# A drain on GpSimd in the expert loop of an encoder layer, between the gathers and the scatter

## The chip, the core and the metric

The kernel runs on one core of a Trainium2 chip. A core has five engines that run their own instruction streams and meet through semaphores: TensorE (PE in the profile, its weight loads PEld), VectorE (DVE), ScalarE (ACT), GpSimd (POOL) and SyncE (SP), beside 16 DMA engines. The metric is the device time of one execution in microseconds.

## What is computed

One layer of an encoder over two sets of 512 tokens, 1024 wide, in float32: attention in two head groups, an output projection, and then a mixture of 16 experts in which each expert picks 64 tokens of each set. The change lies in the last part:

```python
logits = jnp.einsum('nd,de->ne', xf, w_router).astype(jnp.float32)
aff = jax.nn.softmax(logits, axis=-1)
gates, idx = lax.top_k(aff.T, cap)          # cap = 2 * 512 // 16 = 64
xe = xf[idx]
hid = jax.nn.silu(einsum('ecd,edf->ecf', xe, w_gate)) * einsum('ecd,edf->ecf', xe, w_up)
ye = einsum('ecf,efd->ecd', hid, w_down) * gates[..., None]
y = jnp.zeros_like(xf).at[idx.reshape(-1)].add(ye.reshape(-1, d))
x = x + y
```

## The kernel before

The attention, the projection and the routing take the first half of the time. The second half is `experts`, one loop over the 16 experts, written out per engine; the 64 chosen rows of both sets are worked on together, as 128 rows. An expert has 12 chunks of weights of 1 MB (`CHUNKS`): 8 of gate and up, 4 of down.

- SyncE loads each chunk into a ring `raw` (L1471), once the `lo` of the chunk six places earlier is made (`lo_done`).
- ScalarE makes `hi` of it, the value rounded to the matmul's format (L2223), once TensorE has used the slot (`chunk_used`); VectorE makes `lo = raw - hi` (L2301). Both work five chunks ahead of TensorE (`AHEAD`).
- TensorE multiplies each chunk three times, `hi` and `lo` with the two halves of the rows: L2131 to L2133 for gate and up, L2145 to L2147 for down. The down part of expert e - 1 is done in turn e, behind the gate and up part of expert e. A turn has 144 matmuls of 512 columns and 8 transposes (L2108). Gate and up of an expert start when the first half of its `xelo` is there (`xelo_done`).
- The rows of an expert come by four indirect gathers that GpSimd issues, into `xe` (L2065), with indices that a copy has put into `take` (L2060). VectorE transposes `xe` to `xt` (L2317, at j = 5 of its turn, counted by `xt_ready`), ScalarE and VectorE make `xehi` (L2231) and `xelo` (L2312) of that.
- At the end of turn e ScalarE writes `y` of expert e - 1 from the accumulator, times the gates (L2259). It waits for `chunk_used` and for `y_free`. After it come, in ScalarE's order, the `hi` of chunks 5 and 6 of the next turn.
- GpSimd adds `y` to the rows of `out` with an indirect accumulating DMA (L2075), with indices that a copy has put into `give` (L2069). That copy counts `y_free` up. Behind the scatter GpSimd waits until it has landed (`added`).

GpSimd's order in one turn is therefore: wait for `xt_ready` (the transpose has read `xe`, so `xe` may be written again), `take`, four gathers, `give`, wait for `y_done`, scatter, wait for its landing. There is no wait for the gathers' landing on GpSimd; VectorE waits for that, before the next transpose. The loop on GpSimd runs for e = 2 to 14, 13 turns; the gathers of experts 1 and 2 stand before it, two `add_rows` and the two scatters of the last expert (L2100) behind it.

Of the kernel before, what the change touches and what calls it, by code (L numbers as in the profile page):

```python
# [1980 lines left out]
def experts(phase, a, k, moe, ps, banks, out, h2_dram, raw_loaded, route_signals):  # L1981
# [72 lines left out]
    def gpsimd_program(pool):  # L2054
        need_copied, need_free, need_output = (pool.alloc_register(n) for n in ("need_copied", "need_free", "need_output"))

        def gather(e):

            pool.wait_ge(idx_ready, SETS + QUARTERS)
            pool.tensor_copy(moe["take"][:].unsqueeze(2), idx4[:, :, bass.ds(e, 1)]).then_inc(psteps, 1)  # L2060
            pool.reg_mov(need_copied, e)
            pool.wait_ge(idx_ready, SETS + QUARTERS)
            pool.wait_ge(psteps, need_copied)
            for q in range(QUARTERS):
                pool.indirect_dma_start(xe[:, q * PART:(q + 1) * PART], None, h2_quarters,  # L2065
                                        bass.IndirectOffsetOnAxis(moe["take"][:, q:q + 1], 0)).then_inc(xe_loaded, 16)

        def add_rows(e):
            pool.tensor_copy(moe["give"][:], moe["idxT"][:, bass.ds(e, 1)]).then_inc(y_free, 1)  # L2069
            pool.reg_mov(need_free, e + 1)  # L2070
            pool.reg_mov(need_output, 2 * e + 2)
            pool.wait_ge(idx_ready, 2)
            pool.wait_ge(y_free, need_free)
            pool.wait_ge(y_done, need_output)
            pool.indirect_dma_start(out, bass.IndirectOffsetOnAxis(moe["give"][:, 0:1], 0), y[:, :], None,  # L2075
                                    compute_op=ALU.add).then_inc(added, 16)
            pool.wait_ge(added, 16 * e + 16)

        pool.wait_ge(hi_done, 1)
        pool.tensor_tensor(lo[0][:], raw[0][:], hi[0][:].bitcast(F32), ALU.subtract).then_inc(lo_done, 1)  # L2080
        for i in range(2):
            pool.wait_ge(x1_stored[i], 16 * T // 2)
            pool.wait_ge(h2_stored[i], 16 * T // 2)
        pool.wait_ge(idx_ready, 2)
        pool.indirect_dma_start(xe[:, :], None, h2_dram, bass.IndirectOffsetOnAxis(moe["idxT"][:, 0:1], 0)).then_inc(xe_loaded, 16)
        pool.wait_ge(xt_ready, 2)
        gather(1)
        pool.wait_ge(xt_ready, 3)
        gather(2)
        with pool.Fori(2, LAST) as e:  # L2090
            pool.wait_ge(xt_ready, e + 2)
            gather(e + 1)
            add_rows(e - 2)
        add_rows(LAST - 2)
        add_rows(LAST - 1)

        pool.wait_ge(give2_ready, 4)
        for n in range(2):
            pool.wait_ge(y_done, 2 * LAST + n + 1)
            pool.indirect_dma_start(out_halves, bass.IndirectOffsetOnAxis(moe["give2"][:, n:n + 1], 0),  # L2100
                                    y[:, n * BANK:(n + 1) * BANK], None, compute_op=ALU.add).then_inc(added_half, 16)
# [195 lines left out]
    def vector_program(dve):  # L2297
# [91 lines left out]
        low(htlo, hthi, 1, hthi_done, 2 * LAST + 2, htlo_done)  # L2389

    return sync_program, gpsimd_program, tensor_program, scalar_program, vector_program


# [64 lines left out]
```

## Time and profile before

| | us |
|---|---|
| median of 3 runs (1063.44 to 1064.5) | 1064.48 |
| the profiled execution | 1062.62 |
| its span, first to last instruction | 1060.9 |
| busy: TensorE | 1020.0 (96%) |
| busy: VectorE | 892.6 (84%) |
| busy: ScalarE | 780.2 (74%) |
| busy: GpSimd | 499.1 (47%) |
| four gathers and the `take` copy per turn, L2065 and L2060 | 111.0 and 29.0 in all |
| scatters in the turns, L2075 | 24.4 in all |

Engines work side by side, so the busy times don't add up to the span. What counts is which engine has no gap, who waits for whom, and by how much each wait is met early. A row of the timeline gives the start of an instruction, its duration, its engine, line and operands, and in brackets how long the engine had been idle before it and what ended that. A DMA row of GpSimd is the work of issuing it; when the data has landed stands apart. The queue of an engine has a "q" behind the engine's name; drains and semaphore instructions stand there.

### The profile page before, as it was taken

Reading aid. Unit: us, or ns where it says so; the run is one execution under the profiler, and the core shown is the slowest. Engines: PE = TensorE matmul, PEld = TensorE weight load, DVE = VectorE, ACT = ScalarE, POOL = GpSimd, SP = SyncE. Lnnn points to the kernel's source line nnn. Section 1 sums busy time; section 2 is a strip of 40 time slices with the busy share of each in tenths; the row PEclk is TensorE's granted clock in tenths of the full one; section 3 lists DMA queues with packets and bytes.
Section 4 is the critical chain, followed back from the end, with each engine's and each line's share of the span. In section 5 each row is a group of like instructions: output and inputs, shape, how many; then the busy total and the mean of one; then the engine's idle time right before and its main releaser. Section 6 shows DMA issues by size and latency. Waiting matters only on the chain.

```text
span 1060.9 us, 16422 instructions
## 1 busy us (share of the span) xinstructions
PE 1020.0 (96%) x5401; PEld 869.1 (82%) x5401; DVE 892.6 (84%) x1123; ACT 780.2 (74%) x1071; POOL 499.1 (47%) x458
## 2 busy tenths in 40 slices
PE   8999998999999999995999999999999999999995
PEld 7999987888788888884878888888888888888884
DVE  6687669999998954478999999999999999999991
ACT  7655568999999844445678878788787878788771
POOL 2476479555599764554342444234432444324001
PEclk9999999999999999997999999999999999999998
DMA  8132050111322379754999999999999999999972
GB/s 312 62 133 107 1 200 12 50 33 41 111 93 77 87 218 259 210 155 155 332 369 378 405 413 402 402 398 417 403 402 400 399 420 400 403 399 402 419 275 40
DMA packets 62561, 270.30 MB, mean 255 GB/s; under 512 B 12130, under 2 KB 20541, under 8 KB 38701
## 3 DMA queue, kind: packets, MB, share of 16 engines
q1 hardware_dynamic: 56704, 252.34, 62.0%
q0 software_dynamic: 5744, 17.29, 6.5%
q8 instruction: 28, 0.46, 0.2%
q14 instruction: 25, 0.20, 0.1%
q10 hardware_dynamic: 60, 0.01, 0.0%
HBM read 243.27 MB, written 26.35 MB: 254 GB/s over the span
## 4 chain that ended last, share of the span: by engine, by line
PE 47%; DVE 3%; DMA 1%; issue 1%; ACT 0%; POOLq 0%; POOL 0%; DVEq 0%
PE ps L2131 10%; PE ps L2133 10%; PE ps L2132 10%; PE ps L2147 5%; PE ps L2146 5%; PE ps L2145 5%; DVE lo L2301 2%; PE ps L2108 1%; DMA out<-y,give 1%; DMA xe<-h,idxT 0%; DVE idx L1891 0%; DVE affT L1900 0%; DVE gates L1886 0%; POOLq L2404 0%; POOL out L2100 0%
## 5 line engine op out<-in xcount | busy, mean ns | idle before, releaser
L2301 DVE TENSOR_TENSOR lo<-raw,hi 128x2048 fp32r<-128x2048 f32 x191 | 430.9, 2286 | 31.4 <-ACT hi L2223 31.2
L2223 ACT ACTIVATE hi<-raw 128x2048 fp32r<-128x2048 f32 x192 | 364.6, 1918 | 70.0 <-PE ps L2133 58.9
L2131 PE MATMUL ps<-hi,xehi 128*128 128x512 f32 x480 | 188.5, 393 | 1.5 <-DVE h L2323 1.0
L2133 PE MATMUL ps<-hi,xelo 128*128 128x512 f32 x480 | 187.1, 390 | 0.0
L2132 PE MATMUL ps<-lo,xehi 128*128 128x512 f32 x480 | 186.7, 389 | 0.0
L2065 POOL DMA_INDIRECT xe<-h,take x60 | 111.0, 1851 | 25.1 <-issue 13.7
L2060 POOL COPY take<-idx 128x4 uint32 (+1 forms) x15 | 29.0, 1935 | 192.5 <-DVE xt L2317 187.8
L2131 PEld LDWEIGHTS ps<-hi,xehi 128*128 128x128 f32 x480 | 90.3, 188 | 20.5 <-issue 1.4
L2133 PEld LDWEIGHTS ps<-hi,xelo 128*128 128x128 f32 x480 | 90.1, 188 | 19.0
L2132 PEld LDWEIGHTS ps<-lo,xehi 128*128 128x128 f32 x480 | 90.2, 188 | 18.3
L1423 DVE TENSOR_TENSOR probTlo<-ps,probThi 128x512 fp32r<-128x512 f32 x128 | 87.6, 684 | 14.1 <-ACT probThi L1378 11.6
L1369 ACT ACTIVATE prob<-ps,nmax 128x512 f32<-128x512 f32 x128 | 88.8, 693 | 7.9 <-DVE nmax L1427 6.8
L2145 PE MATMUL ps<-hi,hthi 128*128 128x512 f32 x240 | 93.5, 389 | 0.0
L2147 PE MATMUL ps<-hi,htlo 128*128 128x512 f32 x240 | 93.4, 389 | 0.0
L2146 PE MATMUL ps<-lo,hthi 128*128 128x512 f32 x240 | 93.4, 389 | 0.0
L1427 DVE TENSOR_REDUCE nmax<-ps 128x1 f32<-128x512 f32 x128 | 87.3, 683 | 4.4 <-PE ps L1261 2.5
L1274 PEld LDWEIGHTS ps<-ident,prob 128*128 128x128 f32 x512 | 62.7, 141 | 25.6 <-issue 7.9
L1378 ACT ACTIVATE probThi<-ps 128x512 fp32r<-128x512 f32 x128 | 76.8, 600 | 8.5 <-PE ps L1274 7.5
L1274 PE MATMUL ps<-ident,prob 128*128 128x128 f32 x512 | 77.1, 273 | 4.8 <-DVE probTlo L1423 4.4
L2075 POOL DMA_INDIRECT out<-y,give x15 | 24.4, 1629 | 118.0 <-ACT y L2259 118.0
L509 POOL TENSOR_TENSOR small<-small,minus_half 128x1 f32<-128x1 f32 (+4 forms) x40 | 66.1, 1653 | 3.3
L1292 PE MATMUL ps<-probThi,v 128*128 128x256 f32 x256 | 56.3, 301 | 0.0
(302 smaller groups left out, 2189.4 us busy)
## 6 DMA issues: line engine op xcount, KB each, us to landing
raw<-in_w_down SPq DMA_DIRECT2D x64, 1024.0 KB, 7.8
raw<-in_w_gate SPq DMA_DIRECT2D x60, 1024.0 KB, 7.9
raw<-in_w_up SPq DMA_DIRECT2D x60, 1024.0 KB, 7.6
w_raw<-in_w_in SPq DMA_DIRECT2D x8, 592.0 KB, 8.6
x<-in_x SPq DMA_DIRECT2D x8, 512.0 KB, 3.7
r<-reciprocal_sums SPq DMA_DIRECT2D x32, 128.0 KB, 2.9
attention_out<-pj SPq DMA_DIRECT2D x16, 256.0 KB, 2.5
woraw<-in_w_o SPq DMA_DIRECT2D x4, 1024.0 KB, 6.2
```

What stands on the lines that cost most here:

```text
L1274: turned = pe.transpose(ps[:, T_BANKS[u % 2], cols], att["p"][u % 3][:, cols], k["ident"][:])
L1369: act.activation(att["p"][v % 3][:], ps[:, S_BANKS[v % 3], :], ACT.Exp, bias=att["nmax"][:, v:v + 1], accum_out=att["sum"][:, v:v + 1]).th ...
L1423: dve.tensor_tensor(ptlo[v // 2 % 2][:, :, cols], ps[:, T_BANKS[v % 2], :].rearrange("p (a c) -> p a c", a=TS), pthi[v // 2 % 2][:, :, col ...
L2065: pool.indirect_dma_start(xe[:, q * PART:(q + 1) * PART], None, h2_quarters, bass.IndirectOffsetOnAxis(moe["take"][:, q:q + 1], 0)).then_i ...
L2131: pe.matmul(ps[:, dst[n], :], rowhi[:, c, :], hi[w][:, cols], start=c == 0, stop=False)
L2132: pe.matmul(ps[:, dst[n], :], rowhi[:, c, :], lo[w][:, cols], start=False, stop=False)
L2133: last = pe.matmul(ps[:, dst[n], :], rowlo[:, c, :], hi[w][:, cols], start=False, stop=c == KD - 1)
L2145: pe.matmul(ps[:, Y[n], :], hthi[:, f, :], hi[w][:, cols], start=f == 0, stop=False)
L2146: pe.matmul(ps[:, Y[n], :], hthi[:, f, :], lo[w][:, cols], start=False, stop=False)
L2147: last = pe.matmul(ps[:, Y[n], :], htlo[:, f, :], hi[w][:, cols], start=False, stop=f == KD - 1)
L2223: act.activation(hi[s][:], raw[r][:], ACT.Copy).then_inc(hi_done, 1)
L2301: dve.tensor_tensor(lo[s][:], raw[r][:], hi[s][:].bitcast(F32), ALU.subtract).then_inc(lo_done, 1)
```

## The change

GpSimd executes one drain per turn, behind the four gathers of `gather(e + 1)` and ahead of the `give` copy of `add_rows(e - 2)`. A drain holds the instructions behind it until older ones are complete. It carries no semaphore.

```diff
         with pool.Fori(2, LAST) as e:
             pool.wait_ge(xt_ready, e + 2)
             gather(e + 1)
+            pool.drain()
             add_rows(e - 2)
         add_rows(LAST - 2)
         add_rows(LAST - 1)
```

## Rows read from the trace of the kernel before

**Rows 1.** The page's head, its busy table and its chain by engine.
```profile
span 1060.9 us, 16422 instructions
...
PE 1020.0 (96%) x5401; PEld 869.1 (82%) x5401; DVE 892.6 (84%) x1123; ACT 780.2 (74%) x1071; POOL 499.1 (47%) x458
...
PE 47%; DVE 3%; DMA 1%; issue 1%; ACT 0%; POOLq 0%; POOL 0%; DVEq 0%
```

**Rows 2.** Busy time of each engine in one turn, granted clock, DMA share, GB/s.
```profile
607.40:641.10 33.70, 33.70 (x154) 28.05 (x153) 31.69 (x20) 26.90 (x22) 12.66 (x7) 1.00 1.02 404
```

**Rows 3.** Timeline of GpSimd, one turn: start us, us, engine, line, operation.
```profile
584.31 2.05 POOL L2060 COPY take<-idx 128x4 uint32 x1 [13.61 <-DVE xt L2317]
587.15 2.26 POOL L2065 DMA_INDIRECT xe<-h,take  x1 [0.79 <-POOL take L2060]
...
593.47 2.12 POOL L2065 DMA_INDIRECT xe<-h,take  x1 [0.30 <-issue]
595.60 1.42 POOL L2069 COPY give<-idxT 128x1 uint32 x1
602.63 1.63 POOL L2075 DMA_INDIRECT out<-y,give  x1 [5.61 <-ACT y L2259]
617.96 2.06 POOL L2060 COPY take<-idx 128x4 uint32 x1 [13.70 <-DVE xt L2317]
```

**Rows 4.** Timeline of ScalarE at the end of that turn.
```profile
600.53 1.27 ACT L2259 ACTIVATE y<-ps,gT 128x512 f32<-128x512 f32 x2 [0.89 <-PE ps L2147]
601.68 3.72 ACT L2223 ACTIVATE hi<-raw 128x2048 fp32r<-128x2048 f32 x2
```

**Rows 5.** Timeline of TensorE: first matmul of the next turn, first of chunk 5.
```profile
600.24 0.39 PE L2131 MATMUL ps<-hi,xehi 128*128 128x512 f32 x1
...
614.84 0.39 PE L2131 MATMUL ps<-hi,xehi 128*128 128x512 f32 x1
```

**Rows 6.** Timeline of VectorE, from one transpose of the rows to the next.
```profile
582.89 1.24 DVE L2317 STREAM_TRANSPOSE xt<-xe 128x1024 f32<-128x1024 f32 x1
...
588.78 2.29 DVE L2301 TENSOR_TENSOR lo<-raw,hi 128x2048 fp32r<-128x2048 f32 x1 [0.28 <-ACT hi L2223]
...
592.48 4.50 DVE L2301 TENSOR_TENSOR lo<-raw,hi 128x2048 fp32r<-128x2048 f32 x2 [0.20 <-ACT hi L2223]
596.89 1.29 DVE L2312 TENSOR_TENSOR xelo<-xt,xehi 128x512 fp32r<-128x512 f32 x2
...
603.63 4.49 DVE L2301 TENSOR_TENSOR lo<-raw,hi 128x2048 fp32r<-128x2048 f32 x2 [1.05 <-ACT hi L2223]
...
614.34 2.29 DVE L2301 TENSOR_TENSOR lo<-raw,hi 128x2048 fp32r<-128x2048 f32 x1 [0.49 <-ACT hi L2223]
616.55 1.24 DVE L2317 STREAM_TRANSPOSE xt<-xe 128x1024 f32<-128x1024 f32 x1
```

**Rows 7.** Drains at the kernel's end: durations in ns (min/median/max), start in us.
```profile
L2404 POOLq DRAIN  x1: 8731/8731/8731, 1050.5 to 1050.5; - x1
...
L2404 SPq DRAIN  x1: 13/13/13, 1055.7 to 1055.7; - x1
...
L105 POOLq DRAIN  x1: 46/46/46, 1060.6 to 1060.6; - x1
```

**Rows 8.** The last scatter of the kernel on GpSimd, and its landing.
```profile
1050.69 1.56 POOL L2100 DMA_INDIRECT out<-y,give  x1 [1.28 <-ACT y L2294]
...
DMA to landing us min/median/max: 4.8/4.8/4.8
```

**Rows 9.** Landing of the gather that starts at 593.47.
```profile
DMA to landing us min/median/max: 7.2/7.2/7.2
```

**Rows 10.** Timeline of GpSimd behind the loop: `give` copies with an idle engine before them.
```profile
983.14 0.82 POOL L2069 COPY give<-idxT 128x1 uint32<-128x1 uint32 x1 [8.79 <-DMA out<-y,give]
...
1017.13 0.54 POOL L2069 COPY give<-idxT 128x1 uint32<-128x1 uint32 x1 [9.19 <-DMA out<-y,give]
```

**Rows 11.** Landing of the scatter that starts at 602.63.
```profile
DMA to landing us min/median/max: 10.1/10.1/10.1
```

## The prediction

> **What bounds the kernel now.** I read the page's head, its table of busy shares and its chain first: TensorE is busy 96% of the 1060.9 us and carries 47% of the span in the chain, more than all else together [rows 1]. Then the busy time of one turn of the expert loop: TensorE 33.7 of 33.7 us, at a granted clock of 1.00 (the 2.4 GHz level), VectorE 31.7, ScalarE 26.9, GpSimd 12.7, the DMA engines full [rows 2]. So in the loop TensorE is the bound, and a turn lasts what its matmuls last. The period is read from GpSimd's own timeline: its `take` copy starts at 584.31 and again at 617.96, so 33.65 us; I use 33.64 [rows 3].
>
> An edit on GpSimd can then cost only if something late reaches TensorE. So the next question is who waits for GpSimd, and with what margin. In the timeline one turn of GpSimd is: `take` at 584.31, four gathers of which the last runs from 593.47 to 595.59, the `give` copy at 595.60, the scatter at 602.63 [rows 3]. The `give` copy (L2069) increments `y_free`, and ScalarE's write of `y` (L2259) waits for that. ScalarE starts `y` at 600.53 [rows 4], 3.5 us after the copy ended at 597.02. That is GpSimd's slack before it holds anybody. TensorE's nearest margins are these: the first matmul of the turn at 600.24 [rows 5] needs the first half of `xelo`, done at 597.54 (596.89 plus half of the pair) [rows 6]: 2.70 us. Chunk 5 of the same expert, first matmul at 614.84 [rows 5], needs a `lo` that is done at 605.88 [rows 6]: about 9 us.
>
> **The change.** It removes nothing and adds one drain per turn of `Fori(2, LAST)`, 13 in all, between the last gather and the `give` copy. What is queued behind it on GpSimd: the `give` copy with its `y_free`, then the scatter with its DMA, then the wait for that DMA, then the next turn's gathers. Nothing is moved on any other queue. Cost at other engines is zero until `y_free` is late.
>
> How long does such a drain take? The loop shows none, but the end of the kernel does. GpSimd's drain at the end of the block (L2404) began at 1050.5 and took 8.731 us, to 1059.2 [rows 7]. In front of it stood one scatter, already handed over by the sequencer, which ran on GpSimd from 1050.69 to 1052.25 and landed 4.8 us after its start, at 1055.49 [rows 8]. No other engine was awaited: SyncE's own drain was over at 1055.7 [rows 7]. So this drain lasted until 3.7 us after the landing. With nothing outstanding one took 46 ns (L105) [rows 7]. These are the two ends: 0.05 us, or landing plus 3.7 us. The in-loop drain stands right behind four gathers in flight, so it is nearer to L2404's, and I take that: it ends 3.7 us after the last gather lands.
>
> The last gather lands 7.2 us after its start [rows 9], at 593.47 + 7.2 = 600.67. The drain ends at 604.37. Then comes the `give` copy. Behind nothing it took 0.82 and 0.54 us [rows 10]; I take 0.82, with 0.18 to start it (VectorE's transpose ended at 584.13, `take` began at 584.31 [rows 3, 6]) and 0.1 to the waiting ScalarE (second `hi` over by 603.54, `lo` at 603.63 [rows 4, 6]): 1.10 together. `y` can start at 605.47 instead of 600.53: **4.94 us late** in the first turn.
>
> **This lateness feeds itself.** Behind `y` on ScalarE stand the `hi` of chunks 5 and 6 [rows 4], and behind `hi` 5 stands VectorE, which reached `lo` 5 only at 603.63, after waiting 1.05 us for it [rows 6]. From there VectorE works with one gap of 0.49 us until its transpose of `xe` into `xt` ends at 617.79 [rows 6]. And that transpose is what GpSimd waits for before it may gather again: `take` follows at 617.96 [rows 3]. So the late `y` of one turn makes the gathers of the next late, and their landing, and the next `y`. Round the ring, from the end of one transpose to the end of the next: 16.54 us to the landing (584.13 to 600.67), 3.70 of drain, 1.10 of copy, 3.10 from `y` to `lo` 5 (600.53 to 603.63), 13.67 from `lo` 5 to the end of the transpose without the gap: 38.11 us. TensorE's period is 33.64. Before, without the drain, the ring is open: the copy runs while the gathers are still in the air, and its length does not matter.
>
> So the ring becomes the bound. The first `y` is late by 4.94, and each following one by 4.94 - 0.49 = 4.45 more; the 13th by 13 x 4.94 - 12 x 0.49 = 58.34 us. What of it reaches TensorE: `xelo` stands behind `lo` 5 on VectorE with gaps of 0.49, 0.28 and 0.20 us between [rows 6], and then the margin of 2.70: 3.67 us are absorbed once. 58.34 - 3.67 = **54.7 us**. The 9 us at chunk 5 hold: there the new lateness stands against a TensorE that is itself late from the turn before, 4.45 + 3.67 = 8.1. ScalarE catches up within the turn, having 33.7 - 26.9 = 6.8 us to spare [rows 2], and VectorE waits for `hi` 5 in each turn, so its 2.0 us are no second bound. The scatter starts as late as `y`; it landed 10.1 us after 602.63 [rows 11], at 612.7, and the next gather is held by the transpose at 617.8, which is as late: 5.1 us of cover stay. The two `add_rows` after the loop and the tail have no new drain and move with TensorE.
>
> The profiled execution took 1062.62 us, its span 1060.9 and 1.7 around it: 1062.62 + 54.7 = 1117.3. The median of the runs, 1064.48, is 1.9 above the profiled one: **1119 us**.
>
> A rule that speaks against all this: the Trainium skill (VectorE: DVE Perf Modes, section "The DRAIN you can't avoid") calls the drains that are not a VectorE pipe flush boilerplate of constant length, about 12 ns on all five engines. By that rule 13 drains are 0.2 us on GpSimd, hidden, and the time stays at 1064.5. The 46 ns of L105 is of that kind, the 8.731 us of L2404 is not; the trace disagrees where DMAs are outstanding. The skill (Perfetto Trace Analysis, "DMA Instruction — SWDGE (GPSIMD)") also says that a GpSimd DMA ends in the profile when its descriptors are made, not when the data has moved. By that, a drain that asks for ended instructions only would be over at 595.6; the trace agrees with the rule as such (2.12 us beside 7.2 to landing).
>
> **The rivals.** (1) **The drain does not wait for DMAs.** It ends with the last gather's instruction, at 595.6 plus the 0.05 us of L105, `give` still ends before 597.5, and the 3.5 us of slack hide it: 1064.5. More exactly, the ring stays shorter than the period as long as `y` is at most 0.49 us late, that is as long as the drain ends by 599.9, 0.7 us before the landing. Against it: L2404. For it: only that in L2404 something else at the kernel's end may have been counted. (2) **It waits for the landing and no longer.** The first lateness is 600.67 + 1.10 - 600.53 = 1.24; 13 x 1.24 - 5.88 - 3.67 = 6.6 us: 1071. For it: the 3.7 us may belong to the end of the kernel, or to the DMAs that GpSimd had issued since its last drain, many more than the five of a turn, which would then cost little. (3) **Something between.** Counted from the end of the last GpSimd DMA instruction, L2404 took 1059.23 - 1052.25 = 6.98; in the loop that is 602.57, 1.9 past the landing: a first lateness of 3.14, and 13 x 3.14 - 9.55 = 31.3: 1096. The same if the stretched turn, with DMA engines less full, lets gathers land in 4.8 us as at the end instead of 7.2: 54.7 - 13 x 2.4 = 23.5: 1088. (4) **More than 3.7**: if the 3.7 were 1.85 for each of the tail's two scatters, four gathers would cost 7.4: 13 x 8.64 - 9.55 = 102.8: 1167.
>
> **Chances.** Forecast 0.50, (3) 0.22, (2) 0.12, (4) 0.08, (1) 0.08. The range: low end is (2) with the shorter copy, 0.28 x 13 = 3.6 less, 1068; the high end is the forecast with the copy's 1.42 us of the loop [rows 3] for 0.82, 7.8 more, and some for crowding of loads and gathers: 1130. That leaves out (1) and (4). Faster by over 0.2%, about 2 us, which is what a measurement of this kernel can tell from no change: 0.01, since TensorE has no gap in the loop that could close. Same 0.07. Slower 0.92. The forecast's own range is 1105 to 1130.
>
> **What the profile after would show.** A drain row per turn on GpSimd of 8 to 9 us, from the last gather's end to 3.7 us past its landing; `give` about 0.5 to 0.8 us long and released by nothing but the drain; `y` waiting for GpSimd and no longer for TensorE; the distance of two `take` copies 38 us instead of 33.6; VectorE's wait before `lo` 5 grown from 1 us to some 5; TensorE with a gap of about 4.5 us at the first matmul of each turn (L2131, waiting for `xelo`); the DMA rate in the loop down from 404 to about 357 GB/s. Drain rows well under 5 us would make it wrong by rival 1, drains ending at the landing by rival 2. A gap of TensorE at chunk 5 instead of chunk 0 would say that the margins, not the sum, were misread.

## The result

The changed kernel took 1072.52 us (median of 4 runs, 1071.31 to 1072.84), the kernel before 1064.29 in runs beside it (1063.44 to 1064.50): a ratio of 1.008, interval 1.0068 to 1.0092. So it is slower, by 8.2 us, where 54.7 were forecast; 1119 was predicted, and 1072.5 lies near the low end of the range.

The head of the profile after, its busy table and its chain, to be read against [rows 1]:

```profile
span 1070.8 us, 16435 instructions
...
PE 1023.9 (96%) x5401; PEld 868.4 (81%) x5401; DVE 889.4 (83%) x1123; ACT 774.2 (72%) x1071; POOL 490.9 (46%) x458
...
issue 21%; DVE 11%; POOL 10%; PE 4%; POOLq 3%; ACT 3%; DMA 1%; ACTq 0%; DVEq 0%
```

The busy shares have hardly moved, but the chain has: TensorE falls from 47% to 4%, GpSimd, VectorE and ScalarE take its place, and 21% is `issue`, time in which an engine waits for nothing that the profile shows. On GpSimd that is the drain: `issue` is what the profile names ahead of each `give` copy below. The chain is a ring through these three engines, and the timelines show each piece. GpSimd in one turn, to be read against [rows 3]:

```profile
622.37 2.05 POOL L2060 COPY take<-idx 128x4 uint32 x1 [12.98 <-DVE xt L2318]
...
631.16 1.89 POOL L2065 DMA_INDIRECT xe<-h,take  x1 [0.30 <-issue]
638.64 1.44 POOL L2069 COPY give<-idxT 128x1 uint32 x1 [5.60 <-issue]
642.38 1.63 POOL L2075 DMA_INDIRECT out<-y,give  x1 [2.29 <-ACT y L2260]
```

ScalarE at the end of that turn, against [rows 4]:

```profile
640.27 1.27 ACT L2260 ACTIVATE y<-ps,gT 128x512 f32<-128x512 f32 x2 [5.15 <-POOL give L2069]
```

VectorE in the same stretch, against [rows 6]:

```profile
635.56 4.48 DVE L2302 TENSOR_TENSOR lo<-raw,hi 128x2048 fp32r<-128x2048 f32 x2
643.37 4.49 DVE L2302 TENSOR_TENSOR lo<-raw,hi 128x2048 fp32r<-128x2048 f32 x2 [3.33 <-ACT hi L2224]
```

TensorE at the first matmul of a later turn; such a gap did not exist before:

```profile
704.41 0.49 PE L2132 MATMUL ps<-hi,xehi 128*128 128x512 f32 x1 [0.69 <-DVE xelo L2313]
```

The drains of the loop and the one at the kernel's end (durations in ns, starts in us), against [rows 7], and the landing of the gather that starts at 631.16:

```profile
L2093 POOLq DRAIN  x13: 12148/12527/14743, 556.4 to 973.9; - x13
...
L2405 POOLq DRAIN  x1: 5250/5250/5250, 1063.8 to 1063.8; - x1
```

```profile
DMA to landing us min/median/max: 7.1/7.1/7.1
```

The gather lands at 631.16 + 7.1 = 638.26 and `give` starts at 638.64; the drain between them ended at 638.48 (626.33 + 12.15). The `give` copy ends at 640.08, `y` follows at 640.27, 5.15 us after ScalarE was free, VectorE stands idle for 3.33 us instead of 1.05, and `take` comes again 34.6 us after the last. From the first matmul of the experts to the last of the kernel, TensorE takes 551.87 us (510.81 to 1062.68) instead of 540.31 (508.99 to 1049.30): 11.56 more. From there to the end of the span it takes 3.5 us less. 11.56 - 3.5 = 8.1, which is the difference of the medians (8.2). (The profiled execution also began its experts 1.8 us late. Such starts vary from 508.99 to 511.38 among the profiles of this study, with no relation to the drain.)

Two things had to be settled. Why is the ring 34.62 us long, and not 38.1? And why has the end become shorter?

### The profile page after: what moved, and what is told of

The parts are those of the page before. It is cut to its first block, busy times and chain, and to the rows that moved or that the text cites. A ratio compares the mean times of both kernels' runs of the same rounds, so it can differ in the third digit from the quotient of the medians.

```text
span 1070.8 us, 16435 instructions
## 1 busy us (share of the span) xinstructions
PE 1023.9 (96%) x5401; PEld 868.4 (81%) x5401; DVE 889.4 (83%) x1123; ACT 774.2 (72%) x1071; POOL 490.9 (46%) x458
## 4 chain that ended last, share of the span: by engine, by line
issue 21%; DVE 11%; POOL 10%; PE 4%; POOLq 3%; ACT 3%; DMA 1%; ACTq 0%; DVEq 0%
DVE lo L2302 7%; POOL xe L2065 6%; POOLq L2093 3%; ACT hi L2224 3%; POOL take L2060 2%; DVE xt L2318 2%; POOL give L2069 1%; DVE htlo L2307 1%; PE ps L2132 1%; PE ps L2134 1%; PE ps L2133 1%; DMA out<-y,give 1%; DMA xe<-h,idxT 0%; ACT y L2260 0%; PE ps L2148 0%
## 5 line engine op out<-in xcount | busy, mean ns | idle before, releaser
L2224 ACT ACTIVATE hi<-raw 128x2048 fp32r<-128x2048 f32 x192 | 360.0, 1919 | 36.8 <-PE ps L2134 18.0
L2065 POOL DMA_INDIRECT xe<-h,take x60 | 105.7, 1762 | 25.3 <-issue 13.7
L2260 ACT ACTIVATE y<-ps,gT 128x512 f32<-128x512 f32 x30 | 19.0, 685 | 81.6 <-POOL give L2069 77.7
L2069 POOL COPY give<-idxT 128x1 uint32 (+1 forms) x15 | 16.3, 1086 | 94.7 <-issue 77.4
```

What stands on the lines that cost most here:

```text
L2224: act.activation(hi[s][:], raw[r][:], ACT.Copy).then_inc(hi_done, 1)
```

## The experiments

The theories for the loop were these. **Ring**: the drain costs only because `y` waits behind it, and the ring goes on through `hi`, `lo` and the transpose to the next gathers. **Own cost**: a drain costs a sum of its own wherever it stands. And inside the ring, two limits. **L**: the ring is as long as the landing of the gathers plus what follows it. **P**: VectorE itself sets its length, because the `give` copy cannot end before VectorE's instruction. P comes from the rows above: the `give` copy ends at 640.08, and VectorE's pair of `lo` ends at 635.56 + 4.48 = 640.04. In the kernel before it is the same: the copy ended at 597.02 [rows 3], VectorE's first pair of `lo` at 592.48 + 4.50 = 596.98 [rows 6]. It looks as if the copy is held until VectorE's instruction is over.

**The copy ahead of the drain.** The drain stays where the change put it; only the `give` copy, and with it `y_free`, goes ahead of the gathers.

```diff
         with pool.Fori(2, LAST) as e:
+            give_rows(e - 2)
             pool.wait_ge(xt_ready, e + 2)
             gather(e + 1)
             pool.drain()
-            add_rows(e - 2)
+            add_rows(e - 2)          # without the copy
```

> The give copy, with its count of y_free, moves ahead of the wait for xt_ready and the gathers; the drain stays where the change put it, between the gathers and the scatter, and still ends when the last gather has landed. Ring theory (the drain costs only because ScalarE's y waits for the give copy behind it): y waits for TensorE again, the turns are 33.64 us apart, TensorE has no gap in the loop. The drain at the kernel's end takes about 5.2 us instead of 8.7, since the DMAs of the loop are already cleared, so the time is about 1064.3 - 3.5 = 1060.8. Rival (the drain costs by itself: it holds the scatter back, or slows the gathers or other engines): the turns stay at 34.6 us and the time near 1072.

1060.52 us against 1063.66 before, ratio 0.9967 (0.9955 to 0.9979): 3.1 us faster than before, and 11.4 better than the change, each against the kernel before in runs beside it. The drains are as long as in the changed kernel:

```profile
L2096 POOLq DRAIN  x13: 12572/12646/13283, 557.0 to 960.7; - x13
```

And ScalarE's waits over the loop are those of the kernel before, `y` for TensorE alone (each row: what waits, for whom, us in total, times, longest):

```profile
ACT y L2265 <- PE ps L2153: 15.6, 15, 3.1
```

The transposes are 33.64 us apart. Thirteen drains of 12.6 us in the same place cost TensorE nothing once `y` does not wait behind them. Own cost is out, and the ring's link `y_free` is shown.

**The wait without the drain.** GpSimd waits for the gathers' semaphore instead.

```diff
             gather(e + 1)
-            pool.drain()
+            pool.reg_mov(need_landed, GATHERED * (e + 1) + 16)
+            pool.wait_ge(xe_loaded, need_landed)
             add_rows(e - 2)
```

> No drain; in its place GpSimd waits for the semaphore of the four gathers (xe_loaded), so it waits until they have landed and clears nothing. Ring theory: give starts about 0.1 to 0.2 us behind the landing, the turns are 34.4 to 34.5 us apart, TensorE ends its loop some 8 to 10 us later than before, and the end of the kernel keeps its drain of 8.7 us: time 1072 to 1075. Rival (the loss comes from the drain as such, not from the waiting for the landing): time 1064.3.

1075.20 us, ratio 1.0104 (1.0089 to 1.0120): 11.5 us slower than before. The turns are 35.23, 35.35 and 35.58 us long at first and 34.62 from the fourth on, and the old drain stands at the end:

```profile
L2407 POOLq DRAIN  x1: 8731/8731/8731, 1063.6 to 1063.6; - x1
```

So the wait for the landing alone brings the loss in the loop. What the drain does beyond it does not show in the period, which is the same 34.62. It also says that the changed kernel's 8.2 us are some 11.5 lost in the loop and 3.5 won at the end.

**Two drains, and eleven.**

```diff
             gather(e + 1)
+            for _ in range(10):      # 1 in the run with two
+                pool.drain()
             pool.drain()
             add_rows(e - 2)
```

> Two drains in place of one. The second finds nothing in flight. Ring theory: its length d is added to the ring and so 13 times to the time; the rows at the kernel's end say 0.05 us (L105) to 0.29 us (L104), so 0.6 to 3.8 us on top of the changed kernel's 1072.5. Rival (a drain behind a long wait is free, or is limited by something else in the turn): no more than 1072.5.

> Eleven drains in a row instead of one. Two drains gave rows of 0.05 us each 0.02 us apart, so ten more hold GpSimd about 0.7 us longer per turn. Theory P (the give copy ends with VectorE's lo pair whenever it starts before that): it may start up to 1.2 us later at no cost, so turns stay at 34.62 us except where a late landing uses that up, time 1072 to 1074. Theory L (the ring is limited by the landing plus what follows it): turns grow to 35.3 us, time 1080 to 1082.

With two: 1071.43 us, 7.8 over the kernel before (1.0078, 1.0064 to 1.0091), no more than with one. A second drain is a row of 0.05 us:

```profile
L2094 POOLq DRAIN  x13: 47/47/47, 569.7 to 985.6; - x13
```

My ring would have added it 13 times, with the 0.02 us between the two rows; the measurement can't tell 0.9 us, but the period can, and it stayed at 34.62 (after a first turn of 35.23 and a second of 35.58). So the rival in the expectation came out and not the forecast. With eleven: 1070.66 us, 7.2 over (1.0067, 1.0054 to 1.0081), the period 34.62 us behind a first turn of 35.70, in which the ten drains do cost something: it is 35.22 with one. GpSimd's `give` in two turns of that kernel, and VectorE's `lo` pairs beside them:

```profile
638.39 0.58 POOL L2069 COPY give<-idxT 128x1 uint32 x1 [6.46 <-issue]
...
673.37 0.22 POOL L2069 COPY give<-idxT 128x1 uint32 x1 [6.82 <-issue]
```

```profile
634.44 4.48 DVE L2303 TENSOR_TENSOR lo<-raw,hi 128x2048 fp32r<-128x2048 f32 x2
...
669.06 4.48 DVE L2303 TENSOR_TENSOR lo<-raw,hi 128x2048 fp32r<-128x2048 f32 x2
```

The copies end at 638.97 and 673.59, VectorE's pairs at 638.92 and 673.54. The copy starts later and gets shorter by as much; its end stays 0.05 us behind VectorE's. L forecast 1080 and is out; my own 1072 to 1074 for P was a little high as well, where ten more drains took 0.62 us together (0.034 us is the median row).

**The drain itself frees `y`.** The drain carries the count; the copy behind it counts for GpSimd alone.

```diff
-            pool.tensor_copy(moe["give"][:], moe["idxT"][:, bass.ds(e, 1)]).then_inc(y_free, 1)
+            pool.drain().then_inc(y_free, 1)
+            pool.tensor_copy(moe["give"][:], moe["idxT"][:, bass.ds(e, 1)]).then_inc(psteps, 1)
```

> The drain stays between the gathers and the scatter and carries the count of y_free itself; the give copy behind it counts another semaphore, for which only GpSimd waits (the two turns behind the loop get such a drain too). In the changed kernel the give copy that follows the drain ends in most turns 0.04 us behind the end of VectorE's lo pair (640.04 and 640.08), after 0.76 to 1.44 us, where it takes 0.18 with VectorE idle. Theory P (the copy, which reads and writes SBUF, is held until VectorE's instruction with two SBUF inputs ends, and this closes the ring at VectorE's busy time of 31.3 plus 3.3 us = 34.62): with the copy off the way of y, the ring is 16.1 to the landing + 0.2 + 0.2 + 3.1 + 13.5 = 33.1 us, under TensorE's 33.64, so turns are 33.64 apart and the time is 1060 to 1061. Theory L (the ring is limited by the landing of the gathers, as my forecast had it, with an unheld copy): turns are shorter than 34.62 by at most 0.2 us, time 1069 to 1072.

1059.80 us, ratio 0.9963 (0.9949 to 0.9977), 3.7 us under the kernel before. `y` still waits for the landing and the drain, but no longer for the copy:

```profile
636.16 1.49 POOL L2070 COPY give<-idxT 128x1 uint32 x1 [5.55 <-issue]
```

```profile
636.14 1.27 ACT L2260 ACTIVATE y<-ps,gT 128x512 f32<-128x512 f32 x2 [1.49 <-POOLq L2069]
```

`y` starts as `give` starts, with 1.49 us of idle time before it where the kernel before had 0.89 [rows 4]: 0.6 us late. The turns are 33.64 us apart. The landing and the drain are still in the ring, and it is open: what closed it was the copy, up to 1.44 us long. This run alone does not tell a copy that is held from one that is slow. The run with eleven drains does, where the copy gets shorter by as much as it starts later, and L with an unheld copy falls here as well: it forecast 1069 to 1072.

**The transpose one place earlier.** The changed kernel with VectorE's transpose ahead of the `lo` of chunk 9.

```diff
-                if j == GU_CHUNKS - 3 and more:
+                if j == GU_CHUNKS - 4 and more:
                     turn_rows(e + 1)
```

> The changed kernel, with VectorE's transpose of the gathered rows one place earlier in its turn (ahead of the lo of chunk 9 instead of behind it), in every turn of VectorE's loop. GpSimd starts its gathers 2.3 us earlier against TensorE. Ring theory with either limit: landing, drain and give come 2.3 us earlier than y needs them, give ends inside the slack before y as in the kernel before or is at most 1 us late; turns 33.64 us, time 1060 to 1062. Rival (the drain costs a fixed sum per turn, whatever its place in time): 1072.

1059.88 us, ratio 0.9967 (0.9955 to 0.9979). The turns are 33.64 us apart. The same drains, copies and gathers, 2.3 us earlier against TensorE, cost the loop nothing, and `y` starts 0.08 us later than before (0.97 us of idle time for 0.89). The price of the change depends on where in the turn the gathers begin, as a ring's does and a fixed sum doesn't.

**One drain per turn behind the scatter, and one drain in all.**

```diff
             pool.indirect_dma_start(out, ..., compute_op=ALU.add).then_inc(added, 16)
+            pool.drain()             # in the loop; first kernel
             pool.wait_ge(added, 16 * e + 16)
```

```diff
         add_rows(LAST - 2)
+        pool.drain()                 # second kernel, its only one
         add_rows(LAST - 1)
```

> One drain per turn, but behind the scatter instead of ahead of it, beside the wait for the scatter's landing that stands there anyway. It ends about 0.25 us behind that landing, 5 us before the next transpose ends, so nothing waits for it: turns 33.64 us; the drain at the kernel's end takes 5.2 us instead of 8.7: time 1060 to 1061. Rival (13 drains cost in any place): over 1064.

> One drain only, behind the loop, between add_rows(LAST - 2) and add_rows(LAST - 1), where GpSimd idles for 22 us and no DMA of its own is in flight. Theory that a drain clears each GpSimd DMA issued since the drain before it, at some 0.045 us each: this drain takes about 3.5 us, hidden; the one at the kernel's end takes 5.2 us instead of 8.7; time about 1060.8. Rival (the 3.7 us behind the landing belong to the end of the kernel, and in the changed kernel the end was shorter for another reason): this drain takes 0.05 to 0.3 us, the end stays at 8.7 us, time 1064.3.

Behind the scatter: 1059.89 us, 0.9967 (0.9955 to 0.9979), the turns at 33.64. One in all: 1060.55, 0.9972 (0.9961 to 0.9983). Both win the 3.5 us of the end: the last drain took 5.180 and 5.202 us instead of 8.731 [rows 7]. The row of the single drain:

```profile
L2095 POOLq DRAIN  x1: 6687/6687/6687, 1018.6 to 1018.6; - x1
```

It began when the scatter in front of it had landed (1007.05 + 11.5 = 1018.55), so nothing was in flight, and it still took 6.69 us. By then GpSimd had issued 81 DMAs, and no drain since the kernel's start. I had expected 3.5 us: the effect on the time was right, the size of the drain was not. It suggests that such work waits for a drain: between the end of the scatter's instruction (1008.65) and the drain GpSimd had idled for 10 us, and none of it seems to have been done.

**One drain ahead of the loop.**

```diff
         gather(2)
+        pool.drain()
         with pool.Fori(2, LAST) as e:
```

> One drain only, ahead of GpSimd's loop, behind the gathers of expert 2. GpSimd issues 84 DMAs in all; 15 lie before this drain, 69 behind it. Walk theory: a drain goes through every GpSimd DMA issued since the last one, at 6.69 us for 81 (e3) or 0.083 us each, from the moment at which GpSimd is idle, and ends no earlier than the last landing plus 0.2. In the kernel before, the last scatter's work ended at 1052.25 and the drain at 1059.19, 6.94 us for 84. Here 69 take 5.7 us: the drain at the end takes 7.4 to 7.5 us instead of 8.73, time 1.2 to 1.3 us under before. Rival (the end's 3.7 us behind the landing is what counts, and shrinks with the count): 3.7 x 69/84 = 3.0, drain of 8.1 us, time 0.6 under before. Second rival (any drain on the way takes the excess away once for all): 5.2 us, time 3.5 under before. The turns stay at 33.64 us.

1062.45 us, 0.9988 (0.9979 to 0.9998): 1.0 us faster. The time does not separate the first two theories, but it excludes the third. The last drain of that kernel:

```profile
L2405 POOLq DRAIN  x1: 7751/7751/7751, 1051.8 to 1051.8; - x1
```

Its 7.75 us lie between the 7.4 to 7.5 of the walk (a drain goes over every DMA since the last one at 0.083 us each, once) and the 8.1 of the rival, and neither is the rule. What is, the traces show when each drain's end is set against the last landing of a GpSimd DMA before it:

| drain | DMAs issued since the drain before | last landing, us | end of the drain, us | behind the landing, us |
|---|---|---|---|---|
| last, run with one drain in all | 3 | 1056.20 | 1056.37 | 0.17 |
| last, run with drains behind the scatter | 4 | 1055.64 | 1055.85 | 0.21 |
| the changed kernel's loop, third turn (turns 2 to 13: 0.25 to 0.26) | 5 | 638.23 | 638.48 | 0.25 |
| the same, first turn | 19 | 569.24 | 570.07 | 0.83 |
| first behind the scatter | 20 | 580.27 | 581.14 | 0.87 |
| last, this run | 69 | 1056.72 | 1059.59 | 2.87 |
| last, kernel before | 84 | 1055.50 | 1059.19 | 3.69 |
| the single drain, nothing in flight | 81 | 1018.58 | 1025.29 | 6.71 |

The row of the first turn:

```profile
L2093 POOLq DRAIN  x1: 13623/13623/13623, 556.4 to 556.4; - x1
```

The walk fails there. 19 DMAs at 0.083 us are 1.6 us, and the last gather's instruction had ended 5.4 us before its landing, so the walk would have been over long before. But 0.83 us are left. What stands behind a landing is about 0.04 us per DMA, and 0.04 once; with nothing in flight it is twice that, 0.083 per DMA. One sum gives every row: 0.0413 us per DMA is paid twice, first from the start of the drain or from the end of the last DMA instruction, whichever is later, and then again, not before 0.04 us past the last landing. For the kernel before that is 1052.24 + 2 x 84 x 0.0413 = 1059.18 (1059.19 measured), for this run 1056.72 + 0.04 + 69 x 0.0413 = 1059.61 (1059.59), for the single drain 1018.60 + 2 x 81 x 0.0413 = 1025.29. The sum is fitted to these rows, and no run was made to test it. That the count of DMAs, and not of their descriptors or bytes, is what matters was not tried.

## Why the prediction was wrong

**The path of the ring was right.** That `y_free` behind the drain is what hurts, that the lateness returns through `hi`, `lo` and the transpose, that TensorE then waits for `xelo` at the first matmul of a turn, and that the loss grows by a fixed step per turn are what the profile after shows and what the copy ahead of the drain, the earlier transpose and the wait without a drain confirm. What sets the ring's length is another matter (below).

**The step that failed** is the drain's length: "it ends 3.7 us after the last gather lands". It ended 0.25 us after (0.83 in the first turn). L2404's row was the nearest one, but it stood behind 84 DMAs and mine behind five; my rival 2 named that. The 3.7 us were the price of 84 DMAs and not of one drain: at 0.04 us each, five leave 0.25. With 0.25 in place of 3.70 the sum is 54.7 - 13 x 3.45 = 9.8 us, for 11.56 measured. Of the rest 1.35 is one turn of the profiled execution (35.97 us instead of 34.62) in which the third gather took 3.08 us instead of 0.95. Rival 2's own figure, 1071, lies 1.5 under the measured time, and part of that is luck: it has 6.6 us for the loop, where 11.56 were lost, and nothing for the 3.5 won at the end.

**A gain was not in the sum.** The drains in the loop take over what the drain at the end had to do, and that one falls from 8.73 to 5.25 us. I had costed 13 drains and no drain removed; rival 2's reason, followed to the end, would have given it. 1064.5 + 9.8 - 3.5 = 1070.8 would have been the forecast, 1.7 under the measured 1072.5.

**The rest of the ring added up by chance.** I counted 1.10 us for `give` and its two hand-overs. They took 0.16, 1.44 and 0.19. My landing was 0.47 too long (16.54 us from the transpose to the landing; 16.07 were measured, 622.19 to 638.26) and my VectorE stretch 0.22 (13.45, 643.37 to 656.82). The errors cancel: 34.66 by my ring with 0.25, 34.62 measured. But they are not the same thing. The ring as it stands is VectorE's busy time of a turn, 31.3 us, plus one hand-over from `lo` through `give`, `y` and `hi` to `lo`, 3.33. The landing has up to 1.2 us to spare in it, which is why two and eleven drains came free. Where the landing does come later, it takes over, and the copy is short:

```profile
779.74 0.18 POOL L2069 COPY give<-idxT 128x1 uint32 x1 [6.05 <-issue]
```

That is the turn of 35.97 us; VectorE had been done since 773.99 + 4.49 = 778.48, and the copy took 0.18.

The third gather of that turn, and VectorE's `lo` beside it:

```profile
768.42 3.08 POOL L2065 DMA_INDIRECT xe<-h,take  x1 [0.30 <-issue]
768.39 4.48 DVE L2302 TENSOR_TENSOR lo<-raw,hi 128x2048 fp32r<-128x2048 f32 x2
```

In the turn shown at first the same gather starts at 629.91 and takes 0.94 us, and the `lo` pair at 629.89 takes 4.55. Here as there the two start within 0.03 us of each other. In the loop's turns from the second on, the pair is 0.05 to 0.07 us longer where the gather is short, and where the pair keeps its 4.48 us the gather is 2.13 longer. In the runs with the wait, two drains and eleven drains it is the same: three more gathers of 3.08 us (two, one, none), each beside a pair of 4.48, and each ahead of one of the long turns of 35.35 and 35.58 us.

**Rival 1** (the drain does not wait for DMAs) is refuted by each drain row of the loop. What the prediction cites for it from the Trainium skill (VectorE: DVE Perf Modes, section "The DRAIN you can't avoid") is said there of the drains of a kernel's preamble and postamble, not of one that the kernel executes for itself, so its 12 ns were no price for this change. Drains of this study with nothing to do took 0.034 to 0.29 us on GpSimd, those behind its DMAs up to 14.7 us.

**The signs.** Of what the profile after should show, the wait of `y` for GpSimd and TensorE's gap at the first matmul came as named; the sizes did not: 34.6 us between two `take` copies for 38, 3.33 us before `lo` 5 for 5, 0.69 us of gap (2.1 at most) for 4.5, 398 and 384 GB/s in two turns for 357. The drain's end at the landing was the sign named for rival 2. The drain rows are 12 to 15 us long instead of 8 to 9, since a row begins while the gathers ahead of it are still being issued (626.33 in the turn shown).

## What to carry to other kernels

Before adding a wait to an engine, list what its next instruction releases on others: here a 0.2 us copy carried the semaphore that ScalarE needed, and moving that copy ahead of the drain turned 8 us lost into 3 us won. A loop has rings as well as a busiest engine; write out the ring through the new wait and compare its length with the period, because once it is longer the excess is paid in each turn. And a drain of GpSimd at a kernel's end pays for all DMAs that GpSimd has issued since its last drain, so one earlier drain in a place where GpSimd idles anyway took 3.1 us off this kernel, and one per turn behind the scatter 3.6.

## What the runs showed of the hardware

- A drain on GpSimd waits for the landing of GpSimd's own DMAs: 12.1 to 14.7 us in the loop, ending 0.25 us behind the last landing. It also costs time for each DMA issued since the drain before: 0.04 us each behind the landing (0.83 us for 19, 2.87 for 69, 3.69 for 84), and 0.083 each with nothing in flight (6.69 us for 81). A second drain right behind takes 0.05 us.
- A GpSimd copy of 128 x 1 words takes 0.18 us beside an idle VectorE. Started while VectorE runs a `TENSOR_TENSOR` with two inputs in SBUF, it ended 0.04 to 0.05 us behind that instruction, whatever its start: 1.42 us before, 1.44, 0.58 and 0.22 us in the turns shown. In the eleven profiles 159 of these copies started beside such a `lo`, and each ended 0.04 to 0.05 us behind it; the six that started with VectorE idle took 0.18 to 0.19 us. The Trainium skill (SBUF — State Buffer, section "SBUF: two separate sides") says that VectorE and GpSimd share a pair of SBUF ports as an exclusive lock, also for a VectorE instruction with two SBUF inputs against a GpSimd instruction that reads SBUF, and that the one which comes second waits for the whole instruction. The trace agrees, to 0.05 us. In none of these profiles did the copy start beside a VectorE instruction of another kind, so the rule's condition is not shown.
- The third gather's issue took 0.95 us in most turns and 3.08 in one turn of the changed kernel and three turns of the runs like it. Both come where the gather starts within 0.03 us of a `lo`: either the `lo` pair is 0.05 to 0.07 us longer or the gather 2.13 us. That fits the same lock, won by one or the other; no run was made to test it.
